# Six index-query tiles, first modulation sums on TensorE, keys in three passes, late modulation rows spread by a load, fewer rows cleared

## The chip, the cores and the metric

One core of one Trainium2 chip runs the whole program. The metric is the device time of one execution in microseconds; lower is better. Engines: PE is TensorE, DVE VectorE, ACT ScalarE, POOL GpSimd, SP SyncE (it issues most DMAs).

## The reference, cut to what matters

```python
mod = c @ w_ada + b_ada
sh1, sc1, gt1, sh2, sc2, gt2 = split(mod, 6)
h = rmsnorm(x, g_norm_mix) * (1 + sc1) + sh1
proj = h @ w_in                       # qa ka va qi ki wi qb kb vb gb
qi, ki = rope(qi), rope(ki)           # 16 index heads of 64, one key
score[q, s] = sum_h wi[q, h] * relu(qi[q, h] . ki[s] / 8)
sel = top_k(score where chunk(s) <= chunk(q), 256)
y_a = softmax attention of qa over the selected ka, va
y_b = retention(qb, kb, vb) * silu(gb)
x = x + gt1 * (concat(y_a, y_b) @ w_o)
h = rmsnorm(x, g_norm_ffn) * (1 + sc2) + sh2
x = x + gt2 * hier_moe(h)             # top-1 of 4 groups, top-2 of 8 experts
out = rmsnorm(x, g_norm_final)
```

S = 1024 tokens, D = 1024, all float32. A query of the first 256 tokens has at most 256 admissible keys, so for it every admissible key is selected whatever the scores are.

## The kernel before, in words

Tokens are handled in eight tiles of 128 (T = 8), the model dimension in eight pieces k of 128 (KD = 8). Every large product is a `split_product` (L1648 to L1653): both operands are split into a rounded part ("hi", float32r, made by ScalarE) and the rest ("lo", made by VectorE), and TensorE runs three passes, hi x hi, hi x lo, lo x hi. Each engine runs its own instruction list, in the order written; semaphores (`G("name")`) tie them together. The order around the change is the order of these lists.

**Start.** SyncE loads the constants, c, biases, x (4 MB), the key weights, the scale and shift parts of `w_ada` (8 MB) and the weights of projection chunk 0 (L469 to L483). ScalarE squares x for the norm (L752), GpSimd raises to -0.5 (L645), VectorE scales x (L1045), TensorE turns it to hT (L1658) and ScalarE copies it out (L764). VectorE multiplies `w_ada` by c piece by piece (L1054, L1056: partition p holds row p of each piece, so each partition gets a partial sum), and TensorE adds over partitions with a column of ones (L1672). VectorE then applies scale and shift to hT (L1069), in two halves of 512 tokens.

**Keys.** TensorE multiplies the 80 key columns (64 of ki, 16 of wi) by hT in full float32 (L1708), for both halves, before any projection. Later the keys are turned (L1716), rotated (L1135 to L1144), turned back (L1722) and copied to `kiD`.

**Index queries.** `CHUNKS` are blocks of 512 columns of w_in; a unit u is one chunk for one token tile. Units 0 to 15 are qi0 and qi1 for tiles 0 to 7. `project(u)` (24 matmuls) goes to one of four PSUM banks; ScalarE copies the unit out (`a_copy`, L805), VectorE rotates it (`a_rotate`), TensorE turns it (`a_turn`, L1684), VectorE stores it (`a_evacuate`, L1100). ScalarE splits the hT halves and weights between (L790, L783), VectorE makes the rest (L1127, L1118). ScalarE also issues eight DMAs of zeros over `y_dram` here (`zero_rows`, L772), the buffer to which the experts' results are stored.

**Scores.** For tiles 2 to 7 and 16 heads, NU = 96 steps: TensorE (L1752), ScalarE's relu (L830), VectorE's weighted sum (L1169), with three PSUM places. Between steps TensorE makes the four late modulation rows (gt1, sc2, sh2, gt2), `late_products`: eight times, after every twelfth head, eight matmuls (L1737) with c spread over 32 columns, so that the four quarters of 32 partitions of one bank hold four half rows. One buffer; GpSimd loads its two parts (L651) once the step before is done.

**Retention projections.** Units 16 to 47 (qb, kb, vb, gb). VectorE and ScalarE search the top-k thresholds beside them (L845); SyncE stores the results (`b_dram`, L503). Then qa, ka, va with the retention itself (`retain_turn`, `retain_scores`, `retain_values`).

**Attention.** `order` lists what comes between the pairs of heads: `("late", n)` spreads a late half row over 128 partitions by a matmul with ones (L1913) and VectorE adds the bias, which SyncE loaded as 128 equal rows (L1444, L1445, L1447); `("mix", (i, h))` is half of the output product for tile i in bank 7, then VectorE multiplies by gt1 (L1476); `rows`, `norm`, `turn`, `route` follow. The weights w_o are split by ScalarE (L928), VectorE (L1435) and GpSimd (L673). The retained rows come back with L570.

**Experts.** From about 950 us on, one expert block after another is loaded and multiplied; the change does not touch it.

## Time and profile before

| | |
|---|---|
| runs of the kernel before | 1634.56, 1636.85, 1636.9 us (median 1636.85) |
| span of the profiled execution | 1634.3 us (its own time is not given apart from its span) |
| PE, DVE, ACT, POOL busy | 89%, 69%, 56%, 16% of the span |
| bytes moved | 368.01 MB, 225 GB/s on average |

The span runs from the first to the last instruction of one execution that the hardware profiler recorded; the time of a run also has what lies around that. Times in the rows are us from the span's start. "PEclk" is the TensorE clock that was granted, 1.00 for 2.4 GHz and 0.50 for 1.2 GHz. A matmul's record is longer than the distance to the next one, since they are pipelined: distances between starts tell the pace. A full float32 matmul has two records.

### The profile page before, as it was taken

The numbers are of one execution on the slowest core, as the hardware profiler recorded it, in microseconds if no ns is written. First come the engines' busy times: TensorE is split into PE (matmuls) and PEld (weight loads), VectorE is DVE, ScalarE is ACT, GpSimd is POOL, SyncE is SP. The second block draws the span as 40 slices with busy tenths as digits, with TensorE's granted clock in tenths as the row PEclk, the third lists the DMA queues.
The fourth block names the chain that finished last, engine by engine and source line by source line (L and its number), as shares of the span: only waits on it lengthen the run. The fifth ranks groups of instructions, "written<-read, shape, count | busy, mean of one in ns | idle before, by whom it ended". The sixth has DMA issues, their size and how long they took to land.

```text
span 1634.3 us, 21594 instructions
## 1 busy us (share of the span) xinstructions
PE 1460.1 (89%) x7420; PEld 1137.3 (70%) x7420; DVE 1125.2 (69%) x1513; ACT 908.6 (56%) x1224; POOL 268.6 (16%) x191
## 2 busy tenths in 40 slices
PE   3899899999999899788899965999999999999980
PEld 2588445888887787455666654788888888888860
DVE  6732798672247994433344455999999999999967
ACT  5321577878995111323444422777777777777742
POOL 0000110240001000200000001233223223223215
PEclk9899999999999989589999986999999999999995
DMA  9198643213233233311111116999999999999987
GB/s 368 67 330 315 229 155 110 100 66 111 99 117 133 66 129 129 126 52 65 65 52 53 46 52 244 358 394 399 404 401 401 395 397 398 394 404 395 393 325 268
DMA packets 102566, 368.01 MB, mean 225 GB/s; under 512 B 11232, under 2 KB 23648, under 8 KB 77792
## 3 DMA queue, kind: packets, MB, share of 16 engines
q1 hardware_dynamic: 74208, 291.58, 46.8%
q10 hardware_dynamic: 17024, 41.95, 6.7%
q0 software_dynamic: 11264, 33.57, 5.7%
q8 instruction: 42, 0.69, 0.2%
q14 instruction: 28, 0.23, 0.0%
HBM read 306.24 MB, written 69.21 MB: 230 GB/s over the span
## 4 chain that ended last, share of the span: by engine, by line
PE 73%; DVE 14%; ACT 4%; issue 4%; DMA 3%; POOL 2%; SPq 0%; DVEq 0%; ACTq 0%; POOLq 0%
PE PS L1651 19%; PE PS L1653 19%; PE PS L1652 19%; PE PS L1752 3%; PE PS L1775 2%; PE PS L1974 2%; PE PS L1862 2%; PE PS L1849 2%; DMA WK<-in_w_ada 1%; DVE WK L1056 1%; DVE wlo L1497 1%; PE PS L1708 1%; PE PS L1949 1%; DVE ACC L1169 1%; PE PS L1992 1%
## 5 line engine op out<-in xcount | busy, mean ns | idle before, releaser
L1497 DVE TENSOR_TENSOR wlo<-raw,whi 128x2048 fp32r<-128x2048 f32 x192 | 436.3, 2287 | 39.7 <-ACT whi L963 38.0
L963 ACT ACTIVATE whi<-raw 128x2048 fp32r<-128x2048 f32 x192 | 364.0, 1913 | 126.7 <-DVE WK L1580 80.8
L1651 PE MATMUL PS<-whi,xhi 128*128 128x512 f32 x512 | 204.0, 398 | 4.4 <-DVE xlo L1567 3.2
L1653 PE MATMUL PS<-whi,xlo 128*128 128x512 f32 x512 | 201.3, 393 | 0.0
L1652 PE MATMUL PS<-wlo,xhi 128*128 128x512 f32 x512 | 200.3, 391 | 0.0
L845 ACT ACTIVATE KV<-ACC,WK 128x1024 int8<-128x1024 f32 (+4 forms) x160 | 147.5, 926 | 23.7 <-DVE WK L1192 21.1
L1651 PE MATMUL PS<-KVR,BIGR 128*128 128x512 f32 x320 | 126.9, 396 | 1.1 <-ACT WK L830 1.1
L1653 PE MATMUL PS<-KVR,BIGR 128*128 128x512 f32 x320 | 124.9, 390 | 0.0
L1652 PE MATMUL PS<-KVR,BIGR 128*128 128x512 f32 x320 | 124.5, 389 | 0.0
L696 POOL COPY wcol<-tw 128x1 f32 (+1 forms) x32 | 63.0, 1968 | 371.5 <-DVE WK L1601 371.5
L1651 PEld LDWEIGHTS PS<-whi,xhi 128*128 128x128 f32 x512 | 97.2, 190 | 24.7 <-DVE xlo L1567 4.0
L1653 PEld LDWEIGHTS PS<-whi,xlo 128*128 128x128 f32 x512 | 96.7, 189 | 21.0
L1652 PEld LDWEIGHTS PS<-wlo,xhi 128*128 128x128 f32 x512 | 96.8, 189 | 19.3
L1651 PE MATMUL PS<-whi,hhi 128*128 128x512 f32 x256 | 104.3, 407 | 2.7 <-DVE hlo L1572 2.7
L1653 PE MATMUL PS<-whi,hlo 128*128 128x512 f32 x256 | 101.1, 395 | 0.0
L1652 PE MATMUL PS<-wlo,hhi 128*128 128x512 f32 x256 | 100.8, 394 | 0.0
L805 ACT ACTIVATE WK<-PS 128x512 f32<-128x512 f32 x32 | 18.9, 596 | 137.6 <-PE PS L1684 64.7
L1169 DVE SCALAR_TENSOR_TENSOR ACC<-WK,wsc,ACC 128x384 f32<-128x384 f32 (+5 forms) x90 | 85.6, 952 | 10.8 <-ACT WK L830 8.0
L830 ACT ACTIVATE WK<-PS 128x384 f32<-128x384 f32 (+5 forms) x96 | 70.0, 757 | 35.3 <-PE PS L1752 24.4
L1752 PE MATMUL PS<-KV,BIG 64*128 64x512 f32 (+3 forms) x320 | 86.1, 552 | 1.9 <-ACT WK L830 0.9
L920 ACT ACTIVATE WK<-PS 128x512 f32<-128x512 f32 (+3 forms) x48 | 23.7, 541 | 107.2 <-PE PS L1849 107.1
L1476 DVE TENSOR_TENSOR WK<-PS,KV 128x512 f32<-128x512 f32 x16 | 11.1, 692 | 96.2 <-PE PS L1653 96.2
(328 smaller groups left out, 2907.0 us busy)
## 6 DMA issues: line engine op xcount, KB each, us to landing
raw<-in_w_gate SPq DMA_DIRECT2D x64, 1024.0 KB, 7.7
raw<-in_w_up SPq DMA_DIRECT2D x64, 1024.0 KB, 7.6
raw<-in_w_down SPq DMA_DIRECT2D x64, 1024.0 KB, 7.0
y_dram<-zero ACTq DMA_DIRECT2D x8, 3072.0 KB, 11.3
WK<-in_w_ada POOLq DMA_DIRECT2D x16, 1024.0 KB, 7.5
y_dram<-WK ACTq DMA_DIRECT2D x32, 512.0 KB, 6.5
KV<-in_w_in SPq DMA_DIRECT2D x5, 2048.0 KB, 9.4
KV<-in_x SPq DMA_DIRECT2D x16, 512.0 KB, 5.3
```

What stands on the lines that cost most here:

```text
L696: nc.gpsimd.tensor_copy(wcol[:, s:s + 1], column).then_inc(G("m_w"), 1)
L830: own.go(A(WA["R"][:, u % 3, 0:K], PS[:, b:b + 2, :].rearrange("p b c -> p (b c)")[:, 0:K], ACT.Relu), G("sc_relu"))
L845: own.go(A(signs[i], ACC[:, ACC_OFF[i]:ACC_OFF[i] + K], ACT.Sign, bias=sel_try.bitcast(F32)[:, col:col + 1], accum_out=sel_count[:, col:co ...
L963: nc.scalar.activation(whi[:, slot], raw[:, q], ACT.Copy).then_inc(G("m_hi"), 1)
L1169: own(V.scalar_tensor_tensor(acc, R, wsc[:, i, h:h + 1], acc, ALU.mult, ALU.add), G("sc_acc"))
L1497: V.tensor_tensor(wlo[:, slot], raw[:, q], whi[:, slot].bitcast(F32), ALU.subtract)\
L1651: mm(out_, x_hi, w_hi, start=first, stop=False)
L1652: mm(out_, x_hi, w_lo, start=False, stop=False)
L1653: return mm(out_, x_lo, w_hi, start=False, stop=final)
L1752: last = mm(PS[:, 2 * (u % 3) + b, 0:w], qiT[rows, h // 2, tile(i)], kiD[rows, 512 * b:512 * b + w], start=True, stop=True)
L1775: last = mm(PS[:, 2 * (h % 2) + b, 0:w], queries(i)[rows, h // 2, :], kaT[rows, h // 2, 512 * b:512 * b + w], start=True, stop=True)
L1849: last = tr(PS[:, 4 + n % 2, P * (b % 4):P * (b % 4) + P], WC["S"][:, (HA * i + h) % 3, P * b:P * b + P], ident)
```

## The change

1. Only token tiles 2 to 7 are projected for the index queries (12 units, not 16), in the order 4, 5, 6, 7, 2, 3 for qi0. The upper half of the tokens is prepared first. The first four units run together, k by k.
2. The keys' product is a `split_product` with rounded and rest parts of the key weights; its first half stands after the first four units, its second after unit 5.
3. The first modulation sums (scale and shift) are made on TensorE as the late ones are: c spread over 32 columns, four column groups, piece by piece as `w_ada` lands; ScalarE copies the bank (`mod_row`) and sixteen short matmuls turn the four half rows into columns.
4. The constants are loaded in two parts, the second behind the first weights, and the key weights come behind w_ada.
5. The late sums run in 16 steps of one k and two buffers, placed by work (`LATE_AFTER`). The biases are loaded as 32 rows each, VectorE adds them on the rows (`late_rows`), the four rows are stored to `late_dram`, and the loads of gt1, sc2, sh2 and gt2 spread them over 128 partitions. The matmuls and additions of `("late", n)` in the attention are gone; GpSimd multiplies sc2 by g.
6. `zero_rows` clears 32 of the 48 blocks of `y_dram` (the first 16 are always written), and stands in the retention projections.

```diff
-        ada_slot = [BIG[:, 8192:16384].rearrange("p (k c) -> p k c", k=KD),
-                    BIG[:, 16384:24576].rearrange("p (k c) -> p k c", k=KD)]
+        ada_both = BIG[:, 8192:24576].rearrange("p (a k c) -> p a k c", a=2, k=KD)
...
+        IN_ORDER = {0: (4, 5, 6, 7, 2, 3), 1: tuple(SCORED)}
+        UNIT = [(c, t) for c in range(len(CHUNKS)) for t in IN_ORDER.get(c, range(T))]
...
-        LATE_STEPS = 8
+        LATE_STEPS = 2 * KD
         NU = len(SCORED) * NIH
-        LATE_EVERY = NU // LATE_STEPS
...
+        def late_after(n):
+
+            most = (2 * n + 1) * NIH * ACC_ALL // (2 * LATE_STEPS)
+            return next(u for u in range(NU) if sum(P * (FIRST_SCORED + v // NIH + 1) for v in range(u + 1)) >= most)
...
-        between[0] = [[], [], [("late", 0)], [("late", 1)]]
-        between[1] = [[("late", 2)], [("late", 3), ("mix", (0, 0))], [("late", 4), ("mix", (0, 1))],
-                      [("late", 5), ("norm", 0)]]
+        between[0] = [[], [], [], []]
+        between[1] = [[], [("mix", (0, 0))], [("mix", (0, 1))], [("norm", 0)]]
...
-        between[5][2].append(("late", 6))
-        between[5][3].append(("late", 7))
...
+            for k in range(KD):
+                sp.dma_start(ada_both[:, :, k], wada_v[:, 0:2, k]).then_inc(G(f"slot{k // 2}"), 16)
+            _, c0, w = CHUNKS[0]
+            sp.dma_start(W[0][0][:, 0:4], win_v[:, 0:4, c0:c0 + w]).then_inc(G("ld_w0"), 16)
+            sp.dma_start(W[0][0][:, 4:8], win_v[:, 4:8, c0:c0 + w]).then_inc(G("ld_first"), 16)
             sp.dma_start(w_keys, win_v[:, :, KEYS_AT:KEYS_AT + KEYS]).then_inc(G("ld_k0"), 16)
...
+            sp.dma_start(cst[:, early:], const[:, early:]).then_inc(G("ld_rest"), 16)
...
+            sp.wait_ge(G("late_used"), LATE_STEPS)
+            for group in range(2):
+                for rows, row, part in rows_of_group(group):
...
+                if n == RETAIN + 1:
+                    sp.wait_ge(G("late_rows"), 3)
+                    for group in range(2):
+                        for a in range(4):
+                            sp.dma_start(late_dram[2 * group + a // 2:2 * group + a // 2 + 1, 512 * (a % 2):512 * (a % 2) + 512],
+                                         late_sum[group][32 * a:32 * a + 1, :]).then_inc(G("st_late"), 16)
...
-            sp.dma_start(WC["sc2"], b_sc2).then_inc(G("ld_c"), 16)
+            sp.dma_start(WC["sc2"], late_row("sc2")).then_inc(G("ld_c"), 16)
...
+            pool.wait_ge(G("ld_c"), 16 * 4)
+            own(tt(WC["sc2"], WC["sc2"], WC["g"], ALU.mult), G("pool_set"))
...
-                rows = slice(n * MAX_ITEMS // 4 * P, (n + 1) * MAX_ITEMS // 4 * P)
+                fewest = 2 * S // P
+                cleared = (MAX_ITEMS - fewest) // 4
+                rows = slice((fewest + n * cleared) * P, (fewest + (n + 1) * cleared) * P)
...
+            act.wait_ge(G("mod_sum"), 1)
+            own.go(A(W0["row"], PS[:, 0, :], ACT.Copy), G("mod_row"))
...
+            for part in range(4):
+                split_high(0, part)
+                hidden_high(0, (2 * part, 2 * part + 1))
+            act.wait_ge(G("ld_k0"), 16)
+            own.go(A(w_keys_hi, w_keys, ACT.Copy), G("key_hi"))
+            hidden_high(1, range(KD))
+            split_high(1)
...
+                if t in (2, 6):
+                    zero_rows(2 * (n - RETAIN) + t // 4)
...
+            for part in range(4):
+                ks = (2 * part, 2 * part + 1)
+                hidden(0, ks)
+                split_low(0, part)
+                hidden_low(0, ks)
...
+                if m == 5:
+                    rotate_keys()
...
-            for s in range(2):
-                pe.wait_ge(G("mac_done"), s + 1)
-                for k in range(KD):
-                    last = mm(PS[:, s, k:k + 1], W0["mac"][:, s, P * k:P * k + P], ones[:, 0:1], start=True, stop=True)
-                last.then_inc(G("pe_cols"), 1)
+            for k in range(KD):
+                if k % 2 == 0:
+                    pe.wait_ge(G(f"slot{k // 2}"), 32)
+                for g in range(4):
+                    last = mm(PS[32 * g:32 * g + 32, 0, :], cc[:, k:k + 1].to_broadcast([P, 32]),
+                              ada_both[:, g // 2, k, 512 * (g % 2):512 * (g % 2) + 512], start=(k == 0), stop=(k == KD - 1))
+            last.then_inc(G("mod_sum"), 1)
+            pe.wait_ge(G("mod_row"), 1)
+            for g in range(4):
+                for b in range(4):
+                    rows = slice(32 * g, 32 * g + 32)
+                    last = mm(PS[:, g, b:b + 1], W0["row"][rows, P * b:P * b + P], ident[rows, 32 * g:32 * g + 1],
+                              start=True, stop=True)
+            last.then_inc(G("pe_cols"), 1)
...
+            for k in range(KD):
+                pe.wait_ge(G("hT_lo"), k + 1)
+                if k % 2 == 0:
+                    pe.wait_ge(G("w_lo"), k // 2 + 1)
+                for u in range(4):
+                    t = UNIT[u][1]
+                    last = split_product(PS[:, bank_of(u), :], hT_hi[:, k, tile(t)], hT_lo[:, k, tile(t)], W[0][2][:, k],
+                                         W[0][1][:, k], k == 0, k == KD - 1)
+                    if k == KD - 1:
+                        last.then_inc(G("a_proj"), 1)
+            keys_of(0)
...
-                group, k2 = divmod(n, 4)
-                pe.wait_ge(G("ld_late"), 32 * (n + 1))
+                group, k = divmod(n, KD)
+                pe.wait_ge(G(f"ld_late{n % 2}"), 16 * (n // 2 + 1))
```

TensorE's list at the start of the program, before (KV is x, BIG is hT, WK the key weights or the partial sums, ACCR and WKR the two parts of the chunk's weights):

```order
L1658 MATMUL PS<-cst,KV 128x128 x64
L1672 MATMUL PS<-ones,WK 128x1 x16
L1708 MATMUL PS<-BIG,WK 80x512 x16
L1651 MATMUL PS<-ACCR,BIGR 128x512
L1652 MATMUL PS<-WKR,BIGR 128x512
L1653 MATMUL PS<-ACCR,BIGR 128x512
```

And after; BIG at L1720 is w_ada, WK at L1727 the copied rows:

```order
L1705 MATMUL PS<-cst,KV 128x128 x64
L1720 MATMUL PS<-BIG,cc 32x512 x32
L1727 MATMUL PS<-cst,WK 128x1 x16
L1698 MATMUL PS<-ACCR,BIGR 128x512
L1699 MATMUL PS<-WKR,BIGR 128x512
L1700 MATMUL PS<-ACCR,BIGR 128x512
```

Nothing stands any more between the columns and the first projection; the 24 passes of the first half of the keys are entries 100 to 123 of TensorE's list, behind the four units (4 to 99), those of the second half entries 174 to 197.

TensorE's list in the first attention tiles, before, up to the first output product (L1775 query by key, L1849 turning the weights, L1862 values, L1899 and L1906 the `rows` step):

```order
L1862 MATMUL PS<-WK,BIG 64x128 x2
L1913 MATMUL PS<-WK,ones 128x512
L1775 MATMUL PS<-BIG,KV 128x256 x2
L1849 MATMUL PS<-cst,WK 128x128 x2
L1862 MATMUL PS<-KV,BIG 64x128 x2
L1913 MATMUL PS<-WK,ones 128x512
L1899 MATMUL PS<-cst,ssum 64x128 x8
L1906 MATMUL PS<-cst,WK 128x128 x4
...
L1862 MATMUL PS<-KV,BIG 64x128 x4
L1913 MATMUL PS<-WK,ones 128x512
L1651 MATMUL PS<-BIGR,WKR 128x512
```

And after (L1848, L1924, L1937, L1974, L1981 are the same steps):

```order
L1937 MATMUL PS<-WK,BIG 64x128 x2
L1848 MATMUL PS<-BIG,KV 128x256 x2
L1924 MATMUL PS<-cst,WK 128x128 x2
L1937 MATMUL PS<-KV,BIG 64x128 x2
L1974 MATMUL PS<-cst,ssum 64x128 x8
L1981 MATMUL PS<-cst,WK 128x128 x4
...
L1937 MATMUL PS<-KV,BIG 64x128 x4
L1698 MATMUL PS<-BIGR,WKR 128x512
```

The four late matmuls ahead of the output product are gone, and with them VectorE's operations of L1444, L1445 and L1447.

## Rows read from the trace of the kernel before

**Rows 1.** page: span; a group of part 5 (busy us, mean ns | idle before)

```profile
span 1634.3 us, 21594 instructions
L1169 DVE SCALAR_TENSOR_TENSOR ACC<-WK,wsc,ACC 128x384 f32<-128x384 f32 (+5 forms) x90 | 85.6, 952 | 10.8 <-ACT WK L830 8.0
```

**Rows 2.** chain of waits, 0 to 420 us: start us, us, what

```profile
44.98 1.30 DVE WK L1056
...
46.32 3.59 PE PS L1672 x16
...
50.92 16.25 PE PS L1708 x32
```

**Rows 3.** timeline of PE, start: start us, us, engine, line, operation, [idle before]

```profile
30.78 1.06 PE L1658 MATMUL PS<-cst,KV 128*128 128x128 f32 x8 [0.29 <-ACT BIG L764]
...
35.88 3.57 PE L1672 MATMUL PS<-ones,WK 128*128 128x1 f32 x16 [4.04 <-DVE WK L1056]
```

**Rows 4.** timeline of SP, 17 to 19.5 us

```profile
16.82 3.44 SPq L481 DMA_DIRECT2D BIG<-in_w_ada  x1
```

**Rows 5.** DMA issues, 22 to 24: names, count, KB each, us to landing

```profile
BIG<-in_w_ada SPq DMA_DIRECT2D x1, 1024.0 KB, 18.6
```

**Rows 6.** timeline of PE, index queries

```profile
66.60 0.79 PE L1651 MATMUL PS<-ACCR,BIGR 128*128 128x512 f32 x1
...
120.63 0.60 PE L1684 MATMUL PS<-cst,WK 128*128 128x128 f32 x4
...
126.53 0.60 PE L1684 MATMUL PS<-cst,WK 128*128 128x128 f32 x4
...
167.27 4.91 PE L1752 MATMUL PS<-KV,BIG 64*128 64x384 f32 x14 [0.88 <-DVE BIG L1100]
```

**Rows 7.** timeline of PE, scores

```profile
182.66 1.92 PE L1737 MATMUL PS<-WK,cc 128*32 128x512 f32 x16 [1.50 <-DMA WK<-in_w_ada]
...
235.05 13.10 PE L1752 MATMUL PS<-KV,BIG 64*128 64x512 f32 x48
```

**Rows 8.** windows: us, PE, PEld, DVE, ACT, POOL busy, PEclk, DMA share, GB/s

```profile
272.00:448.00 176.00, 175.72 (x775) 145.57 (x776) 84.40 (x215) 147.62 (x313) 31.59 (x24) 1.00 0.28 99
```

**Rows 9.** windows at the start

```profile
35.00:40.00 5.00, 3.57 (x16) 3.49 (x16) 4.86 (x5) 0.00 (x0) 0.00 (x0) 0.51 1.03 394
...
50.00:55.00 5.00, 4.08 (x5) 1.37 (x6) 4.94 (x12) 4.13 (x8) 0.00 (x0) 0.50 0.03 7
```

**Rows 10.** timeline of DVE, 645 to 720

```profile
678.06 0.68 DVE L1444 SCALAR_TENSOR_TENSOR BIG<-PS,BIG 128x512 f32<-128x512 f32 x1
...
682.04 2.36 DVE L1435 TENSOR_TENSOR BIGR<-BIG,BIGR 128x1024 fp32r<-128x1024 f32 x2 [1.76 <-ACT BIGR L928]
```

**Rows 11.** timeline at the start, DVE

```profile
50.23 7.40 DVE L1069 TENSOR_SCALAR BIG<-BIG,mod 128x512 f32<-128x512 f32 x16
60.39 4.91 DVE L1127 TENSOR_TENSOR BIGR<-BIG,BIGR 128x512 fp32r<-128x512 f32 x8 [2.77 <-issue]
65.21 4.62 DVE L1118 TENSOR_TENSOR WKR<-WK,ACCR 128x1024 fp32r<-128x1024 f32 x4
```

**Rows 12.** timeline of DVE, scores

```profile
235.86 16.59 DVE L1169 SCALAR_TENSOR_TENSOR ACC<-WK,wsc,ACC 128x896 f32<-128x896 f32 x14
```

**Rows 13.** landing times by line: stores of L503, then clearings of L772

```profile
DMA to landing us min/median/max: 2.0/2.0/8.2
...
DMA to landing us min/median/max: 9.6/11.3/17.4
```

**Rows 14.** timeline of PE, first attention tiles

```profile
685.25 0.77 PE L1651 MATMUL PS<-BIGR,WKR 128*128 128x512 f32 x1 [2.46 <-DVE BIG L1444]
...
693.39 0.70 PE L1775 MATMUL PS<-BIG,KV 64*128 64x256 f32 x4
...
695.79 1.12 PE L1913 MATMUL PS<-WK,ones 32*128 32x512 f32 x2
```

**Rows 15.** timeline of SP, first attention tiles

```profile
665.70 0.33 SPq L570 DMA_DIRECT2D WK<-yb_dram  x1
```

More of the change, by code:

```diff
@@ L77, in constant_table @@
     lg = np.log1p(-np.exp2(-5.0 - np.arange(HB)))
+    parts["before"] = (p[:, None] < p[None, :])
+    parts["causal"] = (p[None, :] >= p[:, None])
     parts["kfac"] = np.exp(-(p[:, None] + 1.0) * lg[None]) * HD ** -0.5
@@ L513, in _, with late_row @@
             load_rows("g", 3, 0)
+            def late_row(name):
+                n = [row for row, _ in LATE].index(name)
+                return late_dram[n:n + 1, :].to_broadcast([P, D])
             def load_queries(n):
@@ L833, in _ @@
                     split_high(RETAIN, (u - NU // 2) // SPLIT_AT)
-            for group in range(2):
-                act.wait_ge(G("late_used"), LATE_STEPS)
-                own.go(A(late_sum[group], PS[:, 6 + group, :], ACT.Copy, scale=1.0 / 32), G("late_sum"))
             def count_above(n):
```

294 lines of the change are left out of this document (144 added, 150 removed).

## Prediction

> **What bounds the kernel now.** I read the page first: the span is 1634.3 us [rows 1]; the median of the runs, 1636.85, lies 2.55 above it, and the sum is made against the span and carried over to the median. The expert part is not touched, so everything is decided before it, and there the chain of waits tells stage by stage what ends last.
>
> *Start.* The chain runs through VectorE's sixteen multiply-adds of w_ada (the last at 44.98), then the column sums on TensorE (46.32, eight matmuls in 3.59), then the key product in full float32, which holds TensorE for 16.25 us from 50.92 [rows 2]. TensorE had finished turning x at 31.84 [rows 3]. So the start is bound by VectorE. w_ada itself has landed at 20.3 (16.82 + 3.44) + 18.6 = 38.9 [rows 4, 5].
>
> *Index queries.* From the first projection at 66.60 to the first score at 167.27 TensorE never rests; a unit and a turn take 126.53 - 120.63 = 5.90 [rows 6].
>
> *Scores.* VectorE's score sums wait 8.0 us in all for ScalarE's copies [rows 1], which stand behind TensorE, which waits for late w_ada rows: 1.50 us before the group at 182.66 [rows 7]. Otherwise the stage is VectorE's.
>
> *Retention.* TensorE is busy 175.72 of 176 us, the DMA queues 0.28 of the time [rows 8].
>
> *First attention tiles.* A thin chain, mostly at half clock (below).
>
> **The change, part by part.**
>
> *Loads.* 1022 columns of constants (0.52 MB) and the key weights (0.33 MB) now come behind w_ada. At 394 GB/s [rows 9] that is 2.1 us: the last w_ada lands at 36.8.
>
> *Sums on TensorE.* The new products are those of the late rows: eight matmuls took 1.92 us [rows 7], so one k (four) takes 0.96 and eight take 7.7. From about 30.5 (x is turned 1.3 earlier, with the smaller constants ahead of it) six are done by 36.3; the last two end at 36.8 + 1.9 = 38.7. ScalarE's copy of the bank has VectorE's reading of one, 0.68, as its nearest row [rows 10]; 0.9 with the hand-overs (estimate). Then 16 short matmuls where eight took 3.59 at a clock of 0.51 [rows 2, 9]: 3.6 at full clock, 7.2 at half. I take 3.6, because TensorE has paused for 0.9 only, while before it paused from 31.84 to 35.88 [rows 3] ahead of the half clock. Three small VectorE operations, 0.7 (one took 0.3 between 49.91 and 50.23): scale and shift are there at 43.9 instead of 50.2.
>
> *First product.* It no longer waits for all of the keys and halves but for two hT pieces (0.46 each), one weight part (4.62 / 4 = 1.16) and one low piece (4.91 / 8 = 0.61) [rows 11]: 2.8, so it starts at 46.7. VectorE needs 3.3 us for each two k and TensorE 24 x 0.23 = 5.5, so TensorE sets the pace at once, and what follows on VectorE (keys' low part, second half of hT, weights 1: some 14 us) fits under the four tiles' 22 and the keys. But TensorE has idled for over 3 us and starts at half clock: from 50.92 on it stayed at 0.50 until at least 55 [rows 9], which loses 2.4. Start: 49.1 instead of 66.60, **-17.5**. Ends: 5.5 less is saved if sums and columns run at half clock too (1.9 and 3.6 more), 2.4 more is saved if the product runs at full clock.
>
> *Query stage.* Four units fewer: 4 x 5.90 = -23.6. Keys now cost 48 single-pass matmuls here, at most 5.90 / 24 = 0.246 each: +11.8. The copies and rotations (ScalarE, VectorE) stay beside TensorE, and the keys' turns are as before. **-11.8**.
>
> *Scores.* Sixteen steps of one k, two buffers, spaced by work, in place of eight of two k and one buffer. The most is the 8.0 us of VectorE's waiting [rows 1]. But twelve heads of 896 columns and their late group take TensorE 13.10 + 1.92 = 15.0 [rows 7], VectorE 12 x 16.59 / 14 = 14.2 [rows 12]: where waits for loads vanish, TensorE becomes the limit by 0.8 for each twelve heads, some 4.5 over the stage (the 768 tile excepted, where VectorE also splits weights). **-3.5**; ends 0 and -8.0.
>
> *Retention.* Eight bias loads, three VectorE additions of about 0.7, eight one-row stores and eight clearings of 2 MB are moved in. VectorE is busy 84 of 176 [rows 8], SyncE's stores land in 2.0 us [rows 13] and have four buffers, some 17 us of cover: 0. Without that cover each clearing costs what the last rival says. The eight row stores hold SyncE's queue for about 4 us once; the next store is due 6 us later.
>
> *First attention tiles.* Eight 512-column matmuls go, one of which took 1.12 us at full clock [rows 14], the first four about twice that; with them go VectorE's additions of 0.68 [rows 10]. Of the first two little is gained, since the load of yb leaves only at 665.70 [rows 15]; I count 1.4 (estimate). The third's two VectorE operations give another 1.4, so the last low part of w_o, ready at 684.4 now [rows 10], comes at 681.6. The first output product started at 685.25, held by bank 7, and ended at 693.39 [rows 14]: 24 matmuls at 0.34. Now it starts as soon as two parts are there, and at 681.6 fifteen remain, 5.1 us: 686.7, so -6.7. The fifth late step goes before the second half, 1.12 + 0.68: -1.8. **-8.5**, ends -4 and -12. The two at tile 5: **-1.5**. GpSimd now multiplies sc2 ahead of its w_o parts, about 2.3 us after a wait; its parts are needed last and have 5 us.
>
> **Sum:** -17.5 - 11.8 - 3.5 - 8.5 - 1.5 = -42.8: span 1591.5, median **1594**. A measurement of this kernel can tell about 0.2% from no change, 3.3 us.
>
> **Rivals.**
>
> 1. *The start is at half clock throughout.* For: 0.51 from 35 to 40 while TensorE had little to do [rows 9]. Against: it is not idle now. +5.5: 1599.6.
>
> 2. *Small late groups cost as much as large ones.* If a one-k group takes 1.92 like a two-k group [rows 7], eight more bring 15.4 us of TensorE into the scores; less the 8.0 of waits that is a stage 7.4 longer instead of 3.5 shorter. That is 10.9 more than forecast: 1605. Against: the rows after a group show no idle time of TensorE ahead of the next score matmul, as at 235.05 [rows 7]. By the Trainium skill (TensorEngine Tiling (Array Packing), Key Properties) each change of tiling mode drains TensorE, and sixteen more such changes come in. The page gives no price for a drain; at nothing the sum stays, and this rival is what it comes to at the other end.
>
> 3. *The four tiles are not paid out.* Units are counted, but the copies must wait for the turns and the keys' steps stand inside the unit loop of ScalarE and VectorE. If these waits eat the tiles, 23.6 is lost: 1617.6. Against: VectorE is far from busy, with one rotation and one copy in 5.9 us.
>
> 4. *More than forecast:* all 8.0 in the scores and 12 in the tail: 1586.
>
> 5. *Slower: the clearings.* Each now runs beside stores and weight loads on which TensorE depends, on a stage without slack. Before, a clearing of 3 MB took 9.6 to 17.4 us to land [rows 13] while nobody waited. If the eight of them (two thirds as large, 6.4 us at least) stood in front of SyncE's transfers and TensorE had to wait each out, with the queue behind, this passes the gain once each costs over 42.8 / 8 = 5.4 us; at 6.4 to 11.6 it gives 1645 to 1687. Against: 0.28 load, four buffers. The Trainium skill (DMA: Bandwidth & Descriptors, Queues, rings and completion order) has the engines alternate between the rings of SP and ACT, so that a store is not behind a whole clearing. No row here tests it.
>
> **Chances.** Forecast (1588 to 1600 around 1594) 0.60; rival 1 0.13; rival 2 0.10; rival 3 0.05; rival 4 0.10; rival 5 0.02. The range 1583 to 1608 leaves out rivals 3 and 5 and some of the ends, and holds the case that rivals 1 and 2 come halfway together. Faster by over 0.2%: 0.97, within 0.2%: 0.01, slower: 0.02.
>
> **What would show it.** First projection at 46 to 47, at half clock for its first microseconds; a column of 16 short matmuls in 3.6 us; first score near 137; VectorE's waits in the scores below 5 us but TensorE never idle for w_ada; retention still 99% TensorE; first output product starting 8 to 10 us closer to the end of retention. A first product after 52, a retention stage below 98% busy, or a gap at each late group would make me wrong.

## The result, and the profile after

The changed kernel takes **1597.62 us** (median of four runs, 1596.86 to 1599.36), the kernel before 1636.7 beside it (1634.56 to 1636.9): a ratio of 0.9758, 95% interval 0.9744 to 0.9773. The forecast was 1594 in a range of 1583 to 1608. The profiled spans are 1594.8 and 1634.3 us: 39.5 less, where the sum said 42.8.

Where the time went is read best by milestones, the starts of certain rows in the timelines of TensorE and GpSimd:

| start of | before | after | moved by | forecast |
|---|---|---|---|---|
| first projection | 66.60 | 46.25 | -20.35 | 46.7, half clock then |
| first score | 167.27 | 135.68 | -31.6 | -29.3 |
| first retention projection | 272.28 | 241.32 | -31.0 | -32.8 |
| first attention score | 647.50 | 615.05 | -32.5 | -32.8 |
| row sums of tile 1 | 713.29 | 673.12 | -40.2 | -41.3 |
| first gather of the experts | 997.37 | 957.63 | -39.7 | -42.8 |

The start on TensorE (timeline, first rows of the new sums, the short matmuls and the first projection), which answers to [rows 2, 3, 6]:

```profile
31.14 5.36 PE L1720 MATMUL PS<-BIG,cc 128*32 128x512 f32 x48
37.71 1.92 PE L1720 MATMUL PS<-BIG,cc 128*32 128x512 f32 x16 [1.21 <-DMA BIG<-in_w_ada]
40.41 2.47 PE L1727 MATMUL PS<-cst,WK 32*128 32x1 f32 x32 [0.78 <-ACT WK L810]
46.25 0.79 PE L1698 MATMUL PS<-ACCR,BIGR 128*128 128x512 f32 x1 [3.38 <-DVE BIGR L1156]
```

The sums end at 39.6 (38.7 forecast), the short matmuls take 2.5 instead of the 3.6 or 7.2 that I weighed, and the first product starts within 0.5 us of the forecast. The windows, with the granted clock as the third figure from the end, show full clock during the sums, half clock in the first product and again at the first scores (the row at 241 is most of the retention projections, and answers to [rows 8]):

```profile
38.00:40.00 2.00, 1.63 (x16) 0.26 (x8) 0.00 (x0) 0.24 (x1) 0.00 (x0) 1.00 1.05 387
46.00:48.00 2.00, 1.75 (x4) 1.46 (x5) 2.00 (x5) 0.84 (x3) 0.00 (x0) 0.50 1.05 387
50.00:52.00 2.00, 2.00 (x11) 1.59 (x10) 2.00 (x4) 1.45 (x3) 0.00 (x0) 1.00 0.02 7
136.00:138.00 2.00, 2.00 (x7) 0.98 (x5) 0.04 (x1) 0.67 (x2) 0.00 (x0) 0.50 0.80 293
140.00:142.00 2.00, 2.00 (x10) 0.20 (x8) 1.78 (x3) 0.92 (x3) 0.00 (x0) 0.50 0.00 0
142.00:144.00 2.00, 2.00 (x11) 0.85 (x8) 0.20 (x2) 0.71 (x2) 0.72 (x1) 0.99 0.00 0
241.00:417.00 176.00, 175.68 (x775) 145.53 (x776) 83.13 (x217) 146.63 (x311) 31.62 (x24) 1.00 0.54 196
```

Retention is as dense as before, with twice the DMA share (0.54 for 0.28): the clearings are there and TensorE does not wait for them. The scores are the surprise: 105.64 us, where 105.01 stood before and 101.5 was forecast. What TensorE waited for in that stage (list of waits, 135.7 to 243.2, then the same of the kernel before, 167.2 to 273):

```profile
PE PS L1698 <- ACT WK L870: 2.0, 1, 2.0
PE PS L1825 <- DVE BIG L1130: 0.9, 1, 0.9
```

```profile
PE PS L1737 <- DMA WK<-in_w_ada: 2.3, 3, 1.5
PE PS L1651 <- ACT WK L830: 1.1, 1, 1.1
PE PS L1752 <- ACT WK L830: 0.9, 2, 0.6
```

The waits for late parts of `w_ada` are gone, as meant, and with them every wait inside the stage; only its two ends have one. TensorE now has no pause from its first to its last score, and so looks like the limit there. VectorE still waits, for ScalarE, which waits for TensorE (page, then VectorE's timeline and TensorE's late steps in the tile of 1024 columns):

```profile
L1210 DVE SCALAR_TENSOR_TENSOR ACC<-WK,wsc,ACC 128x384 f32<-128x384 f32 (+5 forms) x90 | 85.6, 951 | 9.8 <-ACT WK L870 6.9
```

```profile
228.46 5.25 DVE L1210 SCALAR_TENSOR_TENSOR ACC<-WK,wsc,ACC 128x1024 f32<-128x1024 f32 x4 [0.76 <-ACT WK L870]
234.46 5.25 DVE L1210 SCALAR_TENSOR_TENSOR ACC<-WK,wsc,ACC 128x1024 f32<-128x1024 f32 x4 [0.76 <-ACT WK L870]
```

```profile
218.32 1.06 PE L1810 MATMUL PS<-WK,cc 128*32 128x512 f32 x8
219.31 5.08 PE L1825 MATMUL PS<-KV,BIG 64*128 64x512 f32 x16
```

Four heads and a late step take TensorE 6.0 us and VectorE 5.25.

In the first attention tiles something new stands beside VectorE. GpSimd's product of sc2 and g (L699) waits 9.2 us for the router's weights, and its four w_o parts (L702), which ran from 660.96 to 670.6 before, ahead of VectorE's own, now lie over VectorE's work on tile 0 (timelines of GpSimd and VectorE):

```profile
632.53 2.34 POOL L699 TENSOR_TENSOR BIG<-BIG 128x1024 f32<-128x1024 f32 x1 [9.19 <-DMA wr<-in_w_router]
634.95 9.74 POOL L702 TENSOR_TENSOR BIGR<-BIG,WOR 128x1024 fp32r<-128x1024 f32 x4
```

```profile
637.45 0.69 DVE L1503 TENSOR_TENSOR WKR<-PS,WKR 128x512 fp32r<-128x512 f32 x1 [0.62 <-ACT WKR L971]
638.06 2.10 DVE L1506 TENSOR_TENSOR WKR<-WK,WKR 128x512 fp32r<-128x512 f32 x1
642.61 4.30 DVE L1487 TENSOR_TENSOR BIGR<-BIG,BIGR 128x1024 fp32r<-128x1024 f32 x2 [1.76 <-ACT BIGR L966]
```

L1506 has L1503's size and took three times as long; the two parts of L1487 took 4.30, where their like took 2.36 [rows 10].

### The profile page after: what moved, and what is told of

Its sections match the earlier page's. It is cut to its first block, busy times and chain, and to the rows that moved or that the text cites. A ratio compares the mean times of both kernels' runs of the same rounds, so it can differ in the third digit from the quotient of the medians.

```text
span 1594.8 us, 21442 instructions
## 1 busy us (share of the span) xinstructions
PE 1424.1 (89%) x7372; PEld 1111.2 (70%) x7372; DVE 1096.2 (69%) x1471; ACT 906.3 (57%) x1220; POOL 271.8 (17%) x192
## 4 chain that ended last, share of the span: by engine, by line
PE 75%; DVE 11%; ACT 5%; issue 3%; DMA 3%; POOL 2%; SPq 1%; DVEq 0%; ACTq 0%; POOLq 0%
PE PS L1698 19%; PE PS L1700 19%; PE PS L1699 19%; PE PS L1825 5%; PE PS L2043 2%; PE PS L1848 2%; PE PS L1937 1%; PE PS L1924 1%; DMA BIG<-in_w_ada 1%; DVE wlo L1543 1%; PE PS L1810 1%; ACT WK L931 1%; ACT KV L881 1%; PE PS L2018 1%; PE PS L2061 1%
## 5 line engine op out<-in xcount | busy, mean ns | idle before, releaser
L1543 DVE TENSOR_TENSOR wlo<-raw,whi 128x2048 fp32r<-128x2048 f32 x192 | 436.3, 2287 | 39.7 <-ACT whi L1001 38.1
L1698 PE MATMUL PS<-KVR,BIGR 128*128 128x512 f32 x304 | 120.4, 396 | 2.0 <-ACT WK L870 2.0
L1700 PE MATMUL PS<-KVR,BIGR 128*128 128x512 f32 x304 | 118.6, 390 | 0.0
L1699 PE MATMUL PS<-KVR,BIGR 128*128 128x512 f32 x304 | 118.3, 389 | 0.0
L958 ACT ACTIVATE WK<-PS 128x512 f32<-128x512 f32 (+3 forms) x48 | 23.5, 541 | 103.2 <-PE PS L1924 103.2
L1825 PEld LDWEIGHTS PS<-KV,BIG 64*128 64x128 f32 x320 | 43.2, 190 | 49.5 <-issue 30.1
```

What stands on the lines that cost most here:

```text
L1543: V.tensor_tensor(wlo[:, slot], raw[:, q], whi[:, slot].bitcast(F32), ALU.subtract)\
L1698: mm(out_, x_hi, w_hi, start=first, stop=False)
L1699: mm(out_, x_hi, w_lo, start=False, stop=False)
L1700: return mm(out_, x_lo, w_hi, start=False, stop=final)
L1825: last = mm(PS[:, 2 * (u % 3) + b, 0:w], qiT[rows, h // 2, tile(i)], kiD[rows, 512 * b:512 * b + w], start=True, stop=True)
```

## The experiments

All are edits of the changed kernel, each run beside the kernel before on its chip; ratios are against that. This table holds the stretches of all profiled executions, in us: A, first projection to first score; B, to the first retention projection; C, to the first attention score; D, row sums of tile 0 to the norm of tile 0 (GpSimd's root).

| kernel | median | ratio (95%) | first projection | A | B | C | D | span |
|---|---|---|---|---|---|---|---|---|
| before | 1636.7 | 1 | 66.60 | 100.67 | 105.01 | 375.22 | 42.01 | 1634.3 |
| changed | 1597.62 | 0.9758 (0.9744-0.9773) | 46.25 | 89.43 | 105.64 | 373.73 | 36.30 | 1594.8 |
| pool_after | 1596.15 | 0.9749 (0.9731-0.9767) | 46.87 | 90.24 | 105.89 | 375.36 | 32.58 | 1594.0 |
| warm_scores | 1595.23 | 0.9743 (0.9728-0.9758) | 46.27 | 90.06 | 103.04 | 376.84 | 36.60 | 1596.9 |
| warm_first | 1595.03 | 0.9744 (0.9727-0.9761) | 47.84 | 89.70 | 105.82 | 373.76 | 36.31 | 1596.1 |
| late_out | 1597.26 | 0.9765 (0.9751-0.9779) | 46.31 | 90.01 | 104.07 | 373.78 | 36.41 | 1592.9 |
| tiles8 | 1620.27 | 0.9896 (0.9881-0.9911) | 46.33 | 112.88 | 105.66 | 373.74 | 36.00 | 1618.4 |
| clear_early | 1598.73 | 0.9760 (0.9747-0.9774) | 47.14 | 89.89 | 104.25 | 375.19 | 36.73 | 1597.4 |
| late_few | 1593.45 | 0.9730 (0.9715-0.9745) | 46.22 | 89.23 | 101.11 | 375.36 | 36.67 | 1591.4 |
| late_gap | 1593.77 | 0.9727 (0.9712-0.9742) | 46.25 | 89.82 | 102.25 | 375.31 | 37.40 | 1596.2 |
| early_retain | 1594.29 | 0.9746 (0.9732-0.9759) | 46.39 | 89.38 | 102.21 | 373.77 | 36.43 | 1590.9 |
| best | 1590.95 | 0.9721 (0.9707-0.9735) | 46.30 | 90.17 | 99.90 | 373.77 | 35.26 | 1589.6 |
| loads_front | 1602.41 | 0.9790 (0.9774-0.9806) | 50.45 | 89.09 | 105.67 | 373.75 | 36.29 | 1599.7 |
| late_pairs | 1596.24 | 0.9748 (0.9730-0.9766) | 46.29 | 89.56 | 104.56 | 375.32 | 36.16 | 1593.8 |

Medians of one kernel can be trusted to a microsecond or two; the stretches say more, once the clock is taken out of them. What a stretch lost to it is its length times one less its mean granted clock. A lost 1.8 to 2.9 us in every run of the changed kernel and its edits; without that it is 87.2 to 87.5 in all but tiles8. B has two levels where its start is not edited: it lost 3.2 to 3.4 us in seven profiles (the changed kernel, pool_after, warm_first, tiles8, late_few, loads_front, late_pairs) and 1.7 in three (late_out, clear_early, early_retain), with the same pauses ahead of the first score. In warm_scores, late_gap and best, which fill these pauses, it lost nothing. So 1.5 us of B can come and go with the clock alone; the rows of the changed kernel and of early_retain show it:

```profile
139.00:142.00 3.00, 3.00 (x13) 0.70 (x10) 2.43 (x5) 1.47 (x4) 0.00 (x0) 0.50 0.00 0
139.00:142.00 3.00, 3.00 (x18) 1.11 (x16) 2.60 (x5) 1.45 (x4) 0.51 (x1) 0.99 0.00 0
```

**tiles8: four tiles put back.**

```diff
-        IN_ORDER = {0: (4, 5, 6, 7, 2, 3), 1: tuple(SCORED)}
+        IN_ORDER = {0: (4, 5, 6, 7, 0, 1, 2, 3), 1: tuple(range(T))}
```

> The changed kernel with all eight tiles of queries in both passes of the query stage, as before (four projections, their rotations and transposes more); nothing is left out. Theory (the stage is bound by TensorE, a tile costs its 5.90 us): the stretch from the first projection to the first score grows by 23.6 us from 89.4 to 90.2, the rest stays, and the kernel takes 1621 us (1617 to 1624). Rival (the chain of rotations and transposes behind the last tile was what ended the stage, so tiles are not paid out in full): the stretch grows by less than 18 us.

A grew by 23.45 us (23.7 without what it lost to the clock in either), the kernel by 22.7, and every later stretch stayed. The tiles are paid out in full: rival 3 is dead.

**loads_front: the load order put back.**

```diff
+            sp.dma_start(w_keys, win_v[:, :, KEYS_AT:KEYS_AT + KEYS]).then_inc(G("ld_k0"), 16)
+            sp.dma_start(cst[:, early:], const[:, early:]).then_inc(G("ld_rest"), 16)
             for k in range(KD):
                 sp.dma_start(ada_both[:, :, k], wada_v[:, 0:2, k]).then_inc(G(f"slot{k // 2}"), 16)
```

> The changed kernel with the key weights and the rest of the constants loaded ahead of the eight w_ada parts again; nothing is left out. Theory (the first product is set by w_ada's landing): these 0.9 MB push the modulation sums back by about 2.1 us, the first projection starts at 48.4 instead of 46.25 and the kernel takes 1599.7 us (1598.5 to 1601). Rival (another chain, the transposes and hT, sets the start): less than 0.7 us later.

The first projection came 4.2 us later, and the kernel took 4.8 more. TensorE (timeline, then the window of its last sums, with the granted clock as the third figure from the end):

```profile
30.27 5.53 PE L1720 MATMUL PS<-BIG,cc 128*32 128x512 f32 x48
40.34 3.48 PE L1720 MATMUL PS<-BIG,cc 128*32 128x512 f32 x16 [4.54 <-DMA BIG<-in_w_ada]
```

```profile
40.00:42.00 2.00, 1.66 (x8) 0.40 (x12) 0.00 (x0) 0.00 (x0) 0.00 (x0) 0.53 1.04 384
```

TensorE waits 4.54 us for w_ada ahead of its last two steps, where it waited 1.21, and starts them at 40.34 for 37.71. So the 0.85 MB ahead of w_ada cost 2.6 us of landing, near the 2.2 that the bytes take at 394 GB/s. The other 1.6 is the clock: after the pause of 4.54 the last two steps were granted about half of it and took 3.48 us for 1.92. That w_ada's landing sets the start is shown.

**warm_first: the half clock at the first product.**

```diff
             last.then_inc(G("pe_cols"), 1)
+            for n in range(2):
+                mm(PS[:, 6, 0:480], ident, ada_both[:, 1, n, 0:480], start=True, stop=True)
```

> The changed kernel with two idle products of 480 columns at four passes, ident by a part of w_ada, into bank 6 between the 32 column products and the first projection; nothing is left out. Theory (the first projection runs its first 3.7 us at half the clock because TensorE idles 3.4 us before it): the clock is 1.00 soon after 46.3 and the kernel takes about 1.8 us less (1595.8, from 1594.5 to 1597). Rival (the clock rises no earlier, since TensorE was as slow in the modulation sums before it): no change, 1597 to 1598; if the idle products run over the start of the projection, up to 1 us more.

A stayed at 89.70. The first projection came 1.6 us later, which is not the edit's work: w_ada landed 0.3 later, and the last two steps of the sums, ahead of the idle products, were at half clock here and took 3.25 us for 1.92. The idle products closed most of the gap (0.69 left of 3.38), yet the clock fell (windows):

```profile
42.00:44.00 2.00, 2.00 (x30) 2.00 (x30) 0.00 (x0) 0.89 (x1) 0.00 (x0) 1.00 1.03 358
46.00:48.00 2.00, 1.31 (x3) 0.17 (x1) 2.00 (x4) 1.72 (x3) 0.00 (x0) 0.50 1.05 387
50.00:52.00 2.00, 2.00 (x6) 1.52 (x6) 2.00 (x4) 0.97 (x2) 0.00 (x0) 0.50 0.03 10
```

It was full at 42 to 44 and half again from 45 to 52. The short matmuls (32 records of one column) stand in between; that they are what lets it fall was not tried. The theory's edit failed, and the half clock stays unexplained in its cause. The median (1595.03) is lower than the changed kernel's, but this profile has no stretch that is shorter, and the intervals overlap.

**warm_scores: the half clock at the first scores.**

```diff
+            pe.wait_ge(G("key_dve"), 3)
             for m in range(3):
                 a_turn(TURN1 - 3 + m)
-            pe.wait_ge(G("key_dve"), 3)
+                for n in range((6, 4, 4)[m]):
+                    mm(PS[:, 7, :], hT_hi[:, n, tile(7)], W[1][2][:, n], start=True, stop=True)
```

> The changed kernel with 14 idle products into bank 7 (six, four and four) in the gaps between TensorE's last three groups of query transposes; nothing is left out. Theory (TensorE bounds the score stage from its start, and the stage starts at the lower clock because TensorE idles from 130.7 to 135.7): the granted clock stays at 1.00 from 134 to 144, the first score stays near 135.7, the first retention product comes about 3 us earlier than 241.32 and the kernel takes about 3 us less (1594.6, from 1593.5 to 1596). Rival (ScalarE and VectorE set the pace of this stage): the clock rises but the end of the stage does not move, 1597 to 1598. Second rival (the clock falls anyway): no change in either.

Here it worked: the clock stayed at 1.00 and B fell by 2.6 us. But the kernel's profiled span did not fall, since C grew by 3.1: now the clock fell in the 2.0 us pause before retention (windows), and once more at 475 to 485.

```profile
136.00:138.00 2.00, 2.00 (x9) 0.91 (x8) 0.31 (x2) 0.75 (x2) 0.00 (x0) 1.00 1.05 397
238.00:240.00 2.00, 0.63 (x2) 0.53 (x3) 1.46 (x2) 1.32 (x2) 0.00 (x0) 0.85 0.70 170
240.00:242.00 2.00, 2.00 (x6) 1.61 (x5) 1.66 (x7) 0.20 (x1) 0.00 (x0) 0.50 1.05 410
```

That pause is the same 2.0 us in the changed kernel, where the clock did not fall. So C has steps over all the runs: 373.7 to 373.8 where the clock holds (but for a stretch of some 10 us near 540 that all of them have), 375.2 to 375.4 where it falls once more, 376.8 here, where it falls twice more. The kernel before has the second (375.22, with 0.50 granted at 510 to 512): the 1.5 us by which retention "improved" is that, and no effect of the edit.

**late_out: three of four late products left out**, for k = 1 to 6.

```diff
-                for a in range(4):
+                for a in range(1 if k in range(1, KD - 1) else 4):
```

> The changed kernel without 36 of the 64 late modulation products: of a group of four, only the first is made for k = 1 to 6 (its output rows are then incomplete sums), and all loads stay. TensorE's work in the score stage falls by 36 products of about 0.25 us, 9 us. Theory (TensorE bounds the stage throughout): the stage shrinks by 7 to 9 us of its 105.6, down to the VectorE share of 93 us. Rival (TensorE merely keeps up with ScalarE and VectorE): it shrinks by less than 3 us, and TensorE shows idle time waiting for ScalarE.

B fell by 1.6 us, not 7 to 9, and 1.5 of that is the clock's (B lost 1.7 us to it, for 3.2). This was no answer to my question. A step of one product took as long as one of four had (timeline; the changed kernel's rows stand above):

```profile
217.44 1.04 PE L1810 MATMUL PS<-WK,cc 128*32 128x512 f32 x2
218.42 5.07 PE L1825 MATMUL PS<-KV,BIG 64*128 64x512 f32 x16
```

From start to start 0.98, with four products 0.99. The four write different quarters of 32 partitions, and they run side by side. The Trainium skill says so (TensorE: Matmul & The Clock Gate, Why this matters for your kernels: outputs at partitions 0, 32, 64 and 96 land in distinct column groups, and their matmuls run at the same time); this run agrees, and my expectation had left it out. My edit had removed 36 products and none of TensorE's time.

**late_few: twelve of the sixteen steps reduced to one product of 32 columns.**

```diff
-                for a in range(4):
-                    last = mm(PS[32 * a:32 * a + 32, 6 + group, :], cc[:, k:k + 1].to_broadcast([P, 32]),
-                              ada_late[:, n % 2, a // 2, 512 * (a % 2):512 * (a % 2) + 512],
+                for a in range(4 if k in (0, KD - 1) else 1):
+                    w = 512 if k in (0, KD - 1) else 32
+                    last = mm(PS[32 * a:32 * a + 32, 6 + group, 0:w], cc[:, k:k + 1].to_broadcast([P, 32]),
+                              ada_late[:, n % 2, a // 2, 512 * (a % 2):512 * (a % 2) + w],
```

> The changed kernel in which the late modulation products for k = 1 to 6 of both groups are one product of 32 columns instead of four of 512 (their sums are then incomplete); all loads stay. In the run that only dropped three of four products a step still took 1.04 us (0.99 from start to start in the changed kernel), so the four products of a step run side by side, and only a whole step gives time back: here 12 steps, about 11 us of TensorE time. Theory (TensorE bounds the score stage): the stage of 105.6 us shrinks by 7 to 10 us. Rival (ScalarE and VectorE bound it, TensorE only fills the time): by less than 3 us.

B fell by 4.5 us at the same loss to the clock (3.3 for 3.2), between the two expectations, and then VectorE ran without a gap in the last tile, and TensorE's own waits are back (waits of TensorE; timelines of VectorE and TensorE):

```profile
PE PS L1826 <- ACT WK L870: 0.8, 3, 0.3
```

```profile
218.87 13.17 DVE L1210 SCALAR_TENSOR_TENSOR ACC<-WK,wsc,ACC 128x1024 f32<-128x1024 f32 x10
```

```profile
221.19 0.25 PE L1811 MATMUL PS<-WK,cc 128*32 128x32 f32 x2
221.37 5.08 PE L1826 MATMUL PS<-KV,BIG 64*128 64x512 f32 x16
```

So TensorE does bound the stage, but VectorE stands only some 5 us behind it. Each late step is worth less than its 0.99.

**late_pairs: the same steps two at a time.**

```diff
-                if u in LATE_AFTER:
+                if u in LATE_AFTER and LATE_AFTER[u] % 2:
+                    late_products(LATE_AFTER[u] - 1)
                     late_products(LATE_AFTER[u])
```

> The changed kernel with its 16 late steps issued two at a time (eight places, as before the change, but placed by columns and from two buffers); nothing is left out. Theory (small groups are what the new order is worth, since VectorE's three-deep buffer covers one step of 0.99 us at 1024 columns, whose four relus leave 0.1 to 0.2 us of slack, but not 1.85): a pair makes VectorE wait longer, and the score stage of 105.6 us grows by 1 to 3 us. Rival (the number of steps is what counts, not their grouping, and a pair saves a change of tile shape): the stage stays within 0.5 us or shrinks by up to 1 us (16 steps at 0.99 against eight pairs at 1.85).

B fell by 1.1 us, with the same 3.2 lost to the clock: the rival was right. A pair takes 1.85 (timeline: 213.13 to 214.98), two single steps 1.98:

```profile
213.13 1.92 PE L1810 MATMUL PS<-WK,cc 128*32 128x512 f32 x16
214.98 8.76 PE L1825 MATMUL PS<-KV,BIG 64*128 64x512 f32 x32
```

Spreading the steps finer bought nothing on a TensorE that has no idle time to fill; it cost eight more changes at 0.13 us.

**clear_early: the clearings back in the query stage.**

```diff
             for u in range(TURN1):
                 a_copy(u)
+                if u < 8:
+                    zero_rows(u)
...
-                if t in (2, 6):
-                    zero_rows(2 * (n - RETAIN) + t // 4)
```

> The changed kernel with its eight clearing transfers issued by ScalarE in the query stage again, not in the retention stage; nothing is left out. Theory (the clearings are hidden in either place): no change, 1596 to 1599, and the retention stretch stays between 373 and 377. Rival (beside retention they cost transfers that TensorE waits for): the retention stretch shrinks by over 1 us. Second rival (in the shorter query stage they delay the late w_ada parts and weight loads): up to 3 us more before the first retention product.

No change in the kernel's time (1598.73, intervals overlap). C is the longer of its two values, by the clock at 475 to 485, not shorter. B is 1.4 shorter, though no edit touches it: it lost 1.7 us to the clock for 3.2. The same stretch of retention, without clearings (window; DMA share 0.29 for 0.54):

```profile
241.28:416.00 174.72, 174.72 (x771) 144.67 (x772) 82.76 (x217) 145.40 (x309) 31.61 (x24) 1.00 0.29 102
```

Rival 5 is dead.

**pool_after: GpSimd's product of sc2 and g behind its w_o parts.**

```diff
-            pool.wait_ge(G("ld_c"), 16 * 4)
-            own(tt(WC["sc2"], WC["sc2"], WC["g"], ALU.mult), G("pool_set"))
             for k in range(4, KD):
                 pool.wait_ge(G("w_hi"), 4 * (ATTEND + 3) + WO_ORDER.index(k) + 1)
                 own.go(tt(wo_lo[:, k], wo[:, k], wo_hi[k].bitcast(F32), ALU.subtract), G("wo_lo"))
+            pool.wait_ge(G("ld_c"), 16 * 4)
+            own(tt(WC["sc2"], WC["sc2"], WC["g"], ALU.mult), G("pool_set"))
```

> The changed kernel with GpSimd's product of sc2 and g moved behind its four parts of the w_o split; nothing is left out. Theory (the late product pushed GpSimd's split over VectorE's first output work, where L1506 took 2.10 us against 0.68 of its counterpart before, and L1487 x2 took 4.30 against 2.36): GpSimd's split starts at about 625 instead of 634.95, VectorE's first step is again some 0.7 us and the two parts about 2.4, and the kernel takes about 3 us less than the changed one (1594.5, from 1593 to 1596). Rival (VectorE waited inside these instructions for something else, or another wait takes their place): no change, 1597 to 1598.

D fell by 3.7 us (GpSimd, then VectorE, timelines):

```profile
631.62 9.27 POOL L700 TENSOR_TENSOR BIGR<-BIG,WOR 128x1024 fp32r<-128x1024 f32 x4 [4.98 <-ACT WOR L966]
640.85 2.81 POOL L702 TENSOR_TENSOR BIG<-BIG 128x1024 f32<-128x1024 f32 x1
```

```profile
640.66 0.77 DVE L1506 TENSOR_TENSOR WKR<-WK,WKR 128x512 fp32r<-128x512 f32 x1
644.29 2.36 DVE L1487 TENSOR_TENSOR BIGR<-BIG,BIGR 128x1024 fp32r<-128x1024 f32 x2 [2.17 <-ACT BIGR L966]
```

Behind GpSimd's four parts L1506 took 0.77 and L1487 2.36. In the changed kernel L1503, which reads PSUM and SBUF, kept its 0.69 beside GpSimd, and only those that read two operands from SBUF were held. By the Trainium skill (SBUF — State Buffer, Who interferes with whom) a VectorE instruction with two SBUF inputs contends with a GpSimd instruction that reads SBUF, and whichever comes second is blocked until the first ends. The rows agree: in the changed kernel L1506 began at 638.06, inside GpSimd's second part, which ended near 639.6, and was done 0.6 later. The whole kernel shows less of it (1596.15, within the interval of the changed one), as in this profile C was at its longer value and the start 0.6 later.

**late_gap: two late steps in TensorE's pauses before the scores.**

```diff
-            most = (2 * n + 1) * NIH * ACC_ALL // (2 * LATE_STEPS)
+            most = (2 * n - 3) * NIH * ACC_ALL // (2 * LATE_STEPS - 4)
...
-        LATE_AFTER = {late_after(n): n for n in range(LATE_STEPS)}
+        LATE_AFTER = {late_after(n): n for n in range(2, LATE_STEPS)}
...
-            for m in range(3):
-                a_turn(TURN1 - 3 + m)
-            pe.wait_ge(G("key_dve"), 3)
...
+            pe.wait_ge(G("key_dve"), 3)
+            for m in range(3):
+                a_turn(TURN1 - 3 + m)
+                if m < 2:
+                    late_products(m)
+                else:
+                    for n in range(4):
+                        mm(PS[:, 7, :], hT_hi[:, n, tile(7)], W[1][2][:, n], start=True, stop=True)
```

> The changed kernel with the first two late steps moved into the two gaps of TensorE between the last three groups of query transposes, four idle products in the third gap, and the other 14 steps spread over the score stage; nothing is left out. Theory (TensorE bounds the score stage): the clock stays at 1.00 at its start (worth 2.6 us in the run with idle products alone) and two steps fewer are worth 2 us: the stretch from first score to first retention product is 101 us (100 to 102) instead of 105.6, and the kernel takes 1593.5 us (1592 to 1595.5). Rival: the stage gets no shorter than the 103.0 of the run with idle products, and the kernel takes 1595 to 1597.

B is 102.25, 3.4 less than in the changed kernel and 0.8 less than in warm_scores, where the clock held too, and the kernel took 1593.77. The profiled execution does not show the gain whole (its span is 1596.2): C was at its longer value and D 1.1 more. It would be 101 but for a wait of 1.23 us for the third step's load, which leaves only when the first step is done (timeline):

```profile
141.17 1.06 PE L1806 MATMUL PS<-WK,cc 128*32 128x512 f32 x8 [1.23 <-DMA WK<-in_w_ada]
```

**early_retain: retention without the pause ahead of it.**

```diff
-            pe.wait_ge(G("sc_relu"), NU)
             for u in range(FIRST[RETAIN], FIRST[ATTEND]):
+                m = u - FIRST[RETAIN]
+                if m in (0, 2, 4):
+                    pe.wait_ge(G("sc_relu"), NU - 2 + m // 2)
                 project(u)
```

> The changed kernel in which the first retention projections no longer wait for the last relu: the first two (banks 0 and 1) wait for the third from last, the next two (banks 2 and 3) for the second from last; nothing is left out. Theory (the 2.0 us that TensorE waits for ScalarE before 241.32 is followed by a stage bound by TensorE, so it is paid in full): the first retention product comes 2 us earlier, with no idle time ahead of it, the clock stays at 1.00 there, and the kernel takes 1595.6 us (1594 to 1597). Rival (the retention stage waits for VectorE's last score work anyway, so the gap moves behind the first four projections): no change.

As expected there is no idle time ahead of the first projection, and C is not longer, so the gap did not move behind it. B is 3.4 us shorter; 1.5 of that is the clock's (1.7 lost for 3.2), and 1.9 the edit's, which is the expected 2. The kernel took 1594.29, with an interval that overlaps the changed one's (timeline of TensorE):

```profile
236.05 1.99 PE L1825 MATMUL PS<-KV,BIG 64*128 64x512 f32 x8
237.98 0.50 PE L1698 MATMUL PS<-KVR,BIGR 128*128 128x512 f32 x1
```

**best: the three edits together**, with `late_after` spacing steps 2 to 15 by `(n - 1) * NIH * ACC_ALL // (LATE_STEPS - 1)`.

> Three edits together, nothing left out: the first two late steps in TensorE's gaps before the scores (the third now later, so that it does not wait 1.23 us for its load), GpSimd's product of sc2 and g behind its w_o parts, and the first retention projections on earlier relus. Theory: they are on one chain and add up: the score stage 101 to 102 us instead of 105.6, the gap of 2.0 gone, and 3.7 us less between the row sums of tile 0 and its norm; the kernel takes 1589 us (1586 to 1592). Rival (what is won before the retention is lost again to the clock, which falls in other places): 1592 to 1595.

1590.95 us, ratio 0.9721 (0.9707 to 0.9735) against 0.9758 (0.9744 to 0.9773): the lowest median of all, and faster than both kernels. B is 99.9, 5.7 less. The expectation comes to 99 to 100 for it, since B holds the score stage (101 to 102) and the pause behind it, which is gone; 3.2 of the 5.7 is what B no longer loses to the clock. D fell by 1.0, not 3.7: GpSimd's moved product now stood in front of L1506,

```profile
632.63 2.36 POOL L702 TENSOR_TENSOR BIG<-BIG 128x1024 f32<-128x1024 f32 x1
```

```profile
633.60 1.95 DVE L1506 TENSOR_TENSOR WKR<-WK,WKR 128x512 fp32r<-128x512 f32 x1
```

1.0 us after it had begun. In pool_after L1506 began 0.2 us ahead of it, took 0.77, and it was GpSimd that took longer (2.81 for 2.36). Counted from the first attention score GpSimd's product began at the same 22.5 us in both; L1506 came at 22.3 there and at 23.5 here. Besides, the clock rose later: the window from 645 to 650 was granted 0.58 here, with the first output product under way since 640.55, and in pool_after that product began at 647.24 and had 1.00 from 650 on. An edit that relies on who comes first has to be timed again after every other edit.

## Why the prediction was right, point by point

- **Start (-17.5).** Right, a little small. 46.7 was 46.25; the half clock of the first product lasted until about 50, which lost some 1.8 us for 2.4. The short matmuls took 2.5 us for 3.6. The term "2.1 us by bytes" for the moved loads is near what loads_front shows, 2.6. Yet TensorE could start on the last part of w_ada only at 37.7, 1.2 ahead of the 38.9 that I worked out for the kernel before and not 2.1: w_ada goes in other pieces now, and what of the difference is theirs stays open. That the start is shorter because the key product (16.25 us) and VectorE's sums no longer stand ahead of the first projection is read from the rows; no run puts either back.
- **Query stage (-11.8).** 100.67 to 89.43, -11.2, with 2.0 us lost to the clock in it, nearly all of which the forecast had put under the start. Without it the stage is 13.3 shorter, for 11.8. The tiles are worth what was forecast (23.7 in tiles8, for 23.6), so the keys cost about 10.4 here and not 11.8 (the difference of the two; no run takes the keys out).
- **Scores (-3.5).** Wrong: +0.6. The step that failed is the saving from vanished waits. I had seen that TensorE would become the limit, but took the saving from VectorE's 8.0 us of waiting. It has to be taken from TensorE's idle time: 4.3 us of waits inside and behind the stage before, of which 2.0 are still there at its end. Against these 2.3 stand 1.0 for eight more steps (16 x 0.99 against 8 x 1.85) and a longer half clock at the start: 6.4 us at 0.50 lose 3.2, where before a granted 0.83 over 167 to 177 lost 1.7. That gives +0.2, near the +0.6 measured. The 1.5 of longer half clock is luck of this execution: clear_early, with the same code there, lost 1.7. Without the clock on either side the stage is 0.8 shorter, for a forecast 3.5. The sign that I had named, VectorE's waits below 5 us, did not come (6.9). warm_scores confirms the clock's part (2.6), late_pairs that of the steps (1.1), late_few the limit.
- **Retention (0).** Right; clear_early shows it. The measured -1.5 is the clock's, and luck: it makes up for the 1.5 of the scores.
- **First attention tiles (-8.5).** -7.7 up to the row sums of tile 1. The mechanism came as told, though the first output product stands only 6.9 us closer to the end of retention (30.87 behind it for 37.75), where I had named 8 to 10. And 3.7 us more were there to be had: I had written that GpSimd's parts "are needed last and have 5 us", which looked at who waits for them, not at whom they hold up.
- **Tile 5 (-1.5).** Right, and hidden. Between the row sums of tile 4 and those of tile 5, where the last two late steps stood, the kernel before took 41.65 us and the changed one 39.71, both at full clock (windows, before and after):

```profile
820.69:862.34 41.65, 38.08 (x273) 26.39 (x273) 17.70 (x31) 19.25 (x41) 0.54 (x1) 1.00 0.21 66
782.00:821.71 39.71, 36.04 (x268) 25.79 (x269) 16.23 (x29) 18.05 (x39) 0.54 (x1) 1.00 0.17 55
```

  What hides it from the row sums of tile 1 to the first gather (+0.4) are 1.5 us more between the row sums of tiles 1 and 2, where the clock granted 0.89 for 0.93, and 0.8 more in the tile behind tile 5, where TensorE now waits 1.0 us for ScalarE ahead of the turning of the retained rows (L1981).
- **Rivals.** 1 (half clock throughout the start): no, the sums and most of the short matmuls ran at 1.00. 2 (small groups cost as much as large): no, 0.99 against 1.85, though 0.13 for each split pair is real. 3 and 5: excluded by tiles8 and clear_early. 4 (more in scores and tail): no.

By the milestones, against the sum: 2.3 us more than forecast ahead of the scores and 1.5 more in retention, the latter by the clock; 4.1 less in the scores, 1.5 of it by the clock; 0.8 less in the first tiles, 1.9 less from there to the experts, 0.2 in these. That is 3.2 too little, the difference between 42.8 and the 39.5 of the spans.

## What to carry to other kernels

When a wait goes, take the gain from the idle time of the engine that will be the limit afterwards, not from that of the one which was seen waiting; where that engine has no idle time, finer spreading of extra work buys nothing, and the work has to go into its pauses. Before work is moved on GpSimd, look at what VectorE does at the new time, and not only at who needs the result. And with a clock that falls in some pauses of 2 us and not in others, compare kernels stage by stage between fixed points, and take what each stage lost to the clock out of it: a real gain of 2 us in one stage can be hidden by the clock in the next, and 1.5 us of a stage can vanish with no edit near it.
